# Up and down projections by seven block products in place of eight, with the bias table stored in parts and read back later

## What is computed

```python
def conv_ffn(x, w_up, conv_w, conv_b, w_down):     # x: 512 x 1024
    h = x @ w_up                                    # 1024 x 5632
    h = causal depthwise convolution of width 3 over the tokens, + conv_b
    a, u = jnp.split(h, 2, axis=-1)                 # 2816 columns each
    return (jax.nn.gelu(a, approximate=True) * u) @ w_down   # 2816 x 1024
```

## Time and profile before

| | us |
|---|---|
| median of 3 runs | 2482.78 (2482.14 to 2487.97) |
| the profiled execution, its own time | 2482.47 |
| its span, first to last instruction | 2480.5 |
| PE busy | 2371.9 (96%) |
| DVE busy | 895.6 (36%) |
| ACT busy | 572.9 (23%) |
| mean granted TensorE clock | 0.979 of full |

### The profile page before, as it was taken

How to read it: one execution, slowest core, us unless ns; L and a number is a source line. 1 busy time by engine, 2 the same in 40 slices (tenths; PEclk the granted TensorE clock), 3 DMA queues, 4 the chain that set the end, 5 groups by cost and what they waited for, 6 DMA issues and landing times.

```text
span 2480.5 us, 33541 instructions
## 1 busy us (share of the span) xinstructions
PE 2371.9 (96%) x13710; PEld 1195.7 (48%) x13710; DVE 895.6 (36%) x2187; ACT 572.9 (23%) x1211; POOL 0.2 (0%) x4
## 2 busy tenths in 40 slices
PE   7999999988999999989978999999899998999998
PEld 3555555564444444454434444444444655444553
DVE  6455555541522220034405222210236266131542
ACT  2222222212211110035513111100221253113550
POOL 0000000000000000000000000000000000000000
PEclk9999999979999999999989999999999998999998
DMA  3100000002212121111162212221112110111011
GB/s 113 47 31 31 31 31 31 19 19 104 84 68 85 68 97 70 70 43 43 43 124 102 85 69 83 70 91 70 57 68 83 54 35 35 68 68 63 31 43 68
DMA packets 25264, 154.56 MB, mean 62 GB/s; under 512 B 2476, under 2 KB 2604, under 8 KB 11308
## 3 DMA queue, kind: packets, MB, share of 16 engines
q1 hardware_dynamic: 22032, 145.57, 16.4%
q10 hardware_dynamic: 3100, 7.08, 1.6%
HBM read 146.61 MB, written 6.03 MB: 62 GB/s over the span
## 4 chain that ended last, share of the span: by engine, by line
PE 91%; DVE 5%; DMA 2%; issue 1%; ACT 1%; SPq 0%; DVEq 0%; ACTq 0%
PE banks L1384 23%; PE banks L1146 12%; PE banks L1057 8%; PE banks L1086 7%; PE banks L1744 4%; PE banks L470 3%; PE banks L438 3%; PE banks L1596 2%; PE banks L460 2%; PE banks L1630 2%; PE banks L1608 2%; PE banks L2328 2%; DMA arena<-o_attn 2%; PE banks L575 2%; PE banks L1399 1%
## 5 line engine op out<-in xcount | busy, mean ns | idle before, releaser
L1384 PE MATMUL banks<-arena 128*128 128x512 f32 x1344 | 577.7, 592 | 0.0
L1384 PEld LDWEIGHTS banks<-arena 128*128 128x128 f32 x1344 | 255.0, 190 | 319.6 <-issue 318.7
L1146 PE MATMUL banks<-arena 128*128 128x512 f32 x704 | 303.0, 591 | 0.0
L1439 DVE SCALAR_TENSOR_TENSOR arena<-banks,arena 128x511 f32<-128x511 f32 (+1 forms) x176 | 132.0, 750 | 387.4 <-ACT arena L1422 375.3
L1057 PE MATMUL banks<-arena 128*128 128x512 f32 x512 | 227.8, 606 | 14.6 <-DMA arena<-o_attn 14.6
L1146 PEld LDWEIGHTS banks<-arena 128*128 128x128 f32 x704 | 133.0, 189 | 169.7 <-issue 169.7
L1316 DVE TENSOR_TENSOR arena<-arena 128x512 f32<-128x512 f32 x70 | 48.3, 690 | 408.7 <-ACT arena L1275 405.2
L1422 ACT ACTIVATE arena<-banks,arena 128x512 f32<-128x512 f32 x88 | 68.1, 778 | 474.7 <-PE banks L1384 460.3
L1086 PE MATMUL banks<-arena 128*128 128x512 f32 x384 | 168.3, 595 | 0.0
L1057 PEld LDWEIGHTS banks<-arena 128*128 128x128 f32 x512 | 98.9, 195 | 141.1 <-issue 124.3
L1744 PE MATMUL banks<-arena 128*128 128x512 f32 x256 | 124.6, 614 | 0.0
(11 more groups left out here) (280 smaller groups left out, 2607.2 us busy)
## 6 DMA issues: line engine op xcount, KB each, us to landing
arena<-up SPq DMA_DIRECT2D x44, 1024.0 KB, 4.8
arena<-down SPq DMA_DIRECT2D x16, 1408.0 KB, 6.0
arena<-w_mix SPq DMA_DIRECT2D x8, 1728.0 KB, 7.4
arena<-e_in SPq DMA_DIRECT2D x12, 1024.0 KB, 4.8
arena<-o_in SPq DMA_DIRECT2D x8, 1024.0 KB, 4.8
arena<-w_o SPq DMA_DIRECT2D x4, 1024.0 KB, 4.8
arena<-q SPq DMA_DIRECT2D x8, 512.0 KB, 3.3
arena<-o_attn SPq DMA_DIRECT2D x4, 1024.0 KB, 14.8
```

The costliest lines, as they stand in the source:

```text
L1146: ins = pe.matmul(k.ps[:, j, :], k.ring[s][:, t * P:t * P + P], source[:, t, :], start=t == 0, stop=t == FT - 1)
L1384: ins = pe.matmul(k.ps[:, UP + 2 * s + m, :], k.ring[s][:, (m * KT + t) * P:(m * KT + t + 1) * P], source[:, t, :], start=t == 0, stop=t = ...
L1439: dve.scalar_tensor_tensor(conv[j][:, shift:T], k.ps[:, UP + j, 0:T - shift], k.vec("conv", col + tap), conv[j][:, shift:T], ALU.mult, ALU ...
```

## The change

**Up.** The first 4 slabs of a layer (`PLAIN`) stay as they are. The other 18 are computed by `seven_tensor`: the slab's weights are taken as 2 x 2 blocks (two output tiles by even and odd tiles of the contraction), the activations as 2 x 2 blocks (even and odd tiles by first and second half of the tokens), and seven products of blocks replace eight. Each product is 4 matmuls of 128x256. It needs four sums of weight blocks per slab (`weights_vector`, 128x512 each, DVE), four sums of activation blocks per layer (`turned_vector`, 128x1024 each, DVE), and copies of partial results from PSUM by ACT (`part_scalar`: five of 128x256 per slab), joined by DVE (three of 128x256 per slab). The convolution now reads rows in SBUF in place of PSUM.

**Down.** The class `Down` does the same for pairs of output tiles: four turns per layer, each seven products of 11 matmuls of 128x256. A turn needs both slots of the ring at once. DVE makes four sums of weight blocks of 128x1408 per turn, and, during up, `cross_vector` makes four sums of 128x256 of each pair of activation tiles. `TILES` no longer has the down projections; the bridge behind down squares the tiles in SBUF (`down_squared`).

**The first block's output projection** starts in the last pair: `out_tensor` puts 21 of the 64 matmuls of `w_o` in the places of the fill (8 in the levels, 13 in the scan), in banks 4, 5 and 3, and `tensor_begun` does the other 43.

**Attention.** `turned_tensor(s - 1)` moves ahead of `values_tensor(s - 2)`, in all three attention stages.

**Bias.** `bias_out` becomes four transfers of three rows each, issued by ACT behind each of the first four slabs of up in layer 1; `bias_in` moves behind the bridge after down in layer 1; `late_vector` goes behind the index scores of the third block, and the clearing of `idx` goes to the start of `even_in_vector`.

```diff
@@ class TimeMix
+    OUT = ([(0, t) for t in range(6)] + [(1, t) for t in range(6)] + [(m, 6) for m in range(2)] + [(2, t) for t in range(7)])
+    OUT_BANK = {0: 4, 1: 5, 2: 3, 3: 7}
+    def out_tensor(self, pe):
...
+        pe.wait_ge(self.tail_dve.sem, self.tail_dve.at(t, "gated"))
+        o = (m % 2 * KT + t) * P
+        ins = pe.matmul(k.ps[:, self.OUT_BANK[m], :], k.ring[m // 2][:, o:o + P], k.h[:, t, :], start=t == 0, stop=False)
@@ class Down
+        def product(n, bank, w, x, first, waits):
+            for t in range(FT // 2):
+                waits(t)
+                ins = pe.matmul(ps[:, bank, LO], w[:, t, :], x[:, t, :], start=first and t == 0, stop=t == FT // 2 - 1,
+                                skip_group_check=not first)
...
+            product("P1", 0, self.raw(0, 0), actv[:, 0::2, LO], True, even_ready)
...
+            product("P2", 2, self.raw(0, 1), actv[:, 1::2, LO], True, odd_ready)
...
+            product("P4", 3, self.raw(1, 1), self.t["T4"], True, cross_ready)
+            pe.wait_ge(A.sem, A.at(turn, "p1"))
+            pe.wait_ge(W.sem, W.at(turn, "S4"))
+            product("P6", 0, self.s["S2"], self.t["T2"], False, at_first)
...
+            product("P5", 1, self.s["S1"], self.t["T1"], True, at_first)
+            pe.wait_ge(A.sem, A.at(turn, "u2"))
+            product("P7", 0, self.s["S3"], self.t["T3"], False, at_first)
+            pe.wait_ge(A.sem, A.at(turn, "p5"))
+            product("P3", 1, self.s["S4"], actv[:, 1::2, HI], False, at_first)
@@ class ConvUp
+    def seven_tensor(self, pe, layer, i, s, first=False):
...
+        product("P1", y, a11, k.h[:, 0::2, LO], True)
+        pe.wait_ge(J.sem, J.at(layer, i, s - 2, "c11"))
+        pe.wait_ge(W.sem, W.at(layer, i, s, "S1"))
...
+        product("P5", xa, self.s["S1"], self.t[0], True)
+        pe.wait_ge(A.sem, A.at(layer, i, s, "p1"))
+        pe.wait_ge(W.sem, W.at(layer, i, s, "S2"))
...
+        product("P6", y, self.s["S2"], self.t[1], False)
+        pe.wait_ge(A.sem, A.at(layer, i, s, "p5"))
+        pe.wait_ge(W.sem, W.at(layer, i, s, "S4"))
+        product("P3", xa, self.s["S4"], k.h[:, 1::2, HI], False)
+        pe.wait_ge(A.sem, A.at(layer, i, s, "u2"))
+        pe.wait_ge(W.sem, W.at(layer, i, s, "S3"))
...
+        product("P7", y, self.s["S3"], self.t[2], False)
+        product("P2", xb, a12, k.h[:, 1::2, LO], False)
+        pe.wait_ge(A.sem, A.at(layer, i, s, "u3"))
...
+        product("P4", y, a22, self.t[3], False)
@@ ConvUp, ScalarE's order for one slab
+        if not first:
+            self.part_scalar(act, layer, i0, s0, "c21")
+            self.ident_scalar(act, layer, i0, s0, 0, conv)
+        self.part_scalar(act, layer, i, s, "p1")
+        if not first:
+            self.ident_scalar(act, layer, i0, s0, 1, conv)
+        self.part_scalar(act, layer, i, s, "p5")
+        if not first:
+            self.gelu_scalar(act, layer, i0, s0, conv)
+        self.part_scalar(act, layer, i, s, "u2")
+        self.part_scalar(act, layer, i, s, "u3")
@@ ConvUp, VectorE's order
+        with dve.Fori(0, SEVENS // 2 - 1) as i:
             for s in range(2):
...
+                self.weights_vector(dve, layer, i, s + 1)
+                self.seven_vector(dve, layer, i, s, conv)
+            self.cross_vector(dve, layer, i + PLAIN // 2)
@@ class Attend
             project(s)
+            if 1 <= s <= self.count:
+                self.turned_tensor(pe, s - 1)
             if s >= 2:
                 self.values_tensor(pe, s - 2, lambda n: free(s - 2, n))
-            if 1 <= s <= self.count:
-                self.turned_tensor(pe, s - 1)
@@ class Second
-        act.dma_start(bass.AP(self.scratch.ap().tensor, 0, [[P * 641, 12], [641, P], [1, 640]]),
-                      self.line[0:12, :].unsqueeze(1).broadcast_to([12, P, 640])).then_inc(self.scratch_stored, 16)
+        act.dma_start(bass.AP(self.scratch.ap().tensor, 3 * part * P * 641, [[P * 641, 3], [641, P], [1, 640]]),
+                      self.line[3 * part:3 * part + 3, :].unsqueeze(1).broadcast_to([3, P, 640])).then_inc(self.scratch_stored, 16)
@@ program
-            lin.tensor(pe, "w_o", k.h, 2, lambda t: pe.wait_ge(mix.tail_dve.sem, mix.tail_dve.at(t, "gated")))
+            lin.tensor_begun(pe, mix)
...
-            sec.bias_in(act)
-            up.scalar(act, 1, conv, bridge, 2)
+            up.scalar(act, 1, conv, bridge, 2, lambda part: sec.bias_out(act, part))
```

More of the change, by code:

```diff
@@ L655, in tensor, with last_fill @@
             more = n + 1 < PAIRS
+            def last_fill(count):
+                if not more:
+                    for _ in range(count):
+                        self.out_tensor(pe)
             def level_fill(lv, half):
@@ L1024, in stream @@
                          ).then_inc(k.landed[s], 16)
-TILES = {"w_o": 8, "down0": 8, "o_attn": 8, "down1": 8, "e_in": 28, "e_o": 8, "o_in": 24, "o_o": 8}
+TILES = {"w_o": 8, "o_attn": 8, "e_in": 28, "e_o": 8, "o_in": 24, "o_o": 8}
 BASE = {}
@@ L1069, in tensor, with tensor_begun @@
                 self.slab(pe, name, i, s, source)
+    def tensor_begun(self, pe, mix):
+        k, name = self.k, "w_o"
+        assert not mix.out_left
+        pe.wait_ge(mix.tail_dve.sem, mix.tail_dve.at(PAIRS - 1, "gated"))
+        for m in range(4):
+            for t in range(KT - 1 if m < 3 else 0, KT):
+                o = (m % 2 * KT + t) * P
+                ins = pe.matmul(k.ps[:, mix.OUT_BANK[m], :], k.ring[m // 2][:, o:o + P], k.h[:, t, :], start=t == 0,
+                                stop=t == KT - 1)
+                if m == 3 and t == 0:
+                    k.begun(ins, 1)
+            ins.then_inc(self.summed, 1)
+        for s in range(2):
+            self.slab(pe, name, 1, s, k.h)
     def landed_tensor(self, pe, name, n):
@@ L1425, in pair_scalar, with part_scalar @@
         act.activation(conv[2 * s], conv[2 * s], ACT.Gelu_apprx_tanh).then_inc(self.gelu, 1)
-    def scalar(self, act, layer, conv, bridge, n):
+    def part_scalar(self, act, layer, i, s, name):
+        A, S = self.parts, self.products
+        product, bank = {"p1": ("P1", 0), "p5": ("P5", 1), "u2": ("P6", 0), "u3": ("P7", 0), "c21": ("P4", 0)}[name]
+        act.wait_ge(S.sem, S.at(layer, i, s, product))
+        if name == "c21":
+            act.wait_ge(self.used, i * 2 + (2 + layer * FT + PLAIN + s))
+        A.done(act.activation(self.row[1][:, LO] if name == "c21" else self.part[name], self.k.ps[:, UP + 2 * (s % 2) + bank, LO],
+                              ACT.Copy), name)
@@ new lines, in weights_vector @@
+    def weights_vector(self, dve, layer, i, s, first=False):
+        k, S, W = self.k, self.products, self.weights
+        a11, a12, a21, a22 = self.raw(s % 2)
+        dve.wait_ge(k.landed[s % 2], i * 16 + (TURN[f"up{layer}"] + (PLAIN + s) // 2 + 1) * 16)
+        for name, x, y, op, own, use in (("S1", a21, a22, ALU.add, None, "P5"), ("S2", self.s["S1"], a11, ALU.subtract, "S1", "P6"),
+                                         ("S4", a12, self.s["S2"], ALU.subtract, "S2", "P3"),
+                                         ("S3", a11, a21, ALU.subtract, None, "P7")):
+            if own:
+                dve.wait_ge(W.sem, W.at(layer, i, s, own))
+            if not first:
+                dve.wait_ge(S.sem, S.at(layer, i, s - 1, use))
+            W.done(dve.tensor_tensor(self.s[name], x, y, op), name)
```

338 lines of the change are left out of this document (290 added, 48 removed).

## The result

The changed kernel takes 2408.5 us (median of 4 runs, 2407.9 to 2409.0) beside 2482.8 for the kernel before on the same chip: a ratio of 0.9693, 95% interval 0.9679 to 0.9706. It is faster, as forecast, by 74 us in place of 103; the time lies 5.5 us above the upper end of the range. The profiled execution has a span of 2406.8 us (2480.5 before).

The account below looks back on a forecast made before the run. TensorE was taken to set the time almost everywhere (91% of the chain that ended last). From 2482.5 us, -59.9 - 36.7 + 1.0 - 7.5 - 18.3 + 16 + 0.5 + 1.5 = -103.4 gave 2379 us, range 2356 to 2403.

Parts of the forecast that it names:

- Up and down, TensorE, with waits between products: Seven products for eight save 59.9 us in up and 36.7 in down over two layers; waits between products add 1.0.
- DVE and ACT fit under it: In up, new DVE and ACT work costs nothing; DVE needs 8.6 of 12.1 us a slab.
- down starts without a stall: At the start of down, weight sums end at 14 us, P6 is due at 14.25; cost 0, high 1 us twice.
- The rivals of costly waits: In up and down, waits of 0.14 us for each of 308 products cost 43 us, giving 2422; chance 0.08.
- DVE as the bound: In up, DVE sets the pace at 15.0 us a slab, giving 2483 or more; chance 0.03, including other losses that size.
- The projection begun in the last pair: First block: 21 of 64 `w_o` matmuls moved into the last pair save 7.5 us; low 5, high 12.
- The store taken away from `o_attn`: Without the bias store, `o_attn` loses its slab waits and runs like `w_o`: 18.3 us off.
- Attention order and the bias read back: Transposes ahead of values in attention add 1.5 us; reading the bias back beside slabs of `e_in` adds 0.5.
- The bias store put into up: In up of layer 1, four parts delay slabs on three engines: 16 us on, 5 to 35 likely; chance 0.55.
- Its pace of 0.25 to 0.3 us for a row's copy: Bias store in up of layer 1: 0.25 to 0.3 us per copy, the parts lasting some 130 us in all.

Follow-up runs that it names:

- sums done twice: 96-row kernel with each of the four sums of weight blocks per slab done a second time in both up projections; 2376.6 us, ratio 0.9558.
- the experiment: 96-row kernel with none of the output projection `w_o` begun in the last pair; 2369.1 us, ratio 0.9536.
- four-parts-of-12-rows kernel: Changed kernel with the four bias stores in the same places, each of 12 rows with 32 copies instead of 3 with 128; 2376.7 us, ratio 0.9579.
- no part is held: Changed kernel with all four parts in up of layer 1, spaced so each is issued when the one ahead has ended; 2398.2 us, ratio 0.9639.
- 96-row kernel: Changed kernel with the bias row on 96 partitions, stored ahead of `o_attn` by one transfer of 96 rows with 16 copies; 2364.4 us, ratio 0.9530.
- the one with ScalarE held by 22, 27 and 18 copies: 96-row kernel with ScalarE held in up of layer 1 by in-place copies (17.6, 21.7, 14.4 us), without transfers; 2408.8 us, ratio 0.9676.

## Why the prediction was wrong by 29 us

By its own steps, with starts of stages in the two traces:

- *Up and down, TensorE, with waits between products.* Predicted for a layer -29.9 - 18.4 + 0.5 = -47.8. From the start of up to the first matmul of the norm behind down in layer 0: 459.7 before, 411.9 after, -47.8. That a product's wait costs next to nothing, that DVE and ACT fit under it, and that down starts without a stall is right in both layers. The rivals of costly waits and of DVE as the bound are excluded; with sums done twice DVE still costs only 0.27 us a slab. Of DVE's operations the prediction counts 18 in a slab where its own list has 14 (4 + 3 + 4 + 1 + 2), as the kernel has; this changes neither the sum nor which way the rival fell.
- *The projection begun in the last pair.* Predicted -7.5. Up of layer 0 starts at 611.7 in place of 616.8, -5.1; the experiment gives 3.9 in the traces and 4.7 by the medians. So it lies at the low end of 5, or just under it.
- *The store taken away from `o_attn`.* Predicted -18.3. From its start to the start of up it is 82.8 before and 68.1 after: -14.7. No slab is late, but the clock is 0.5 from 1171.8 to 1185.4, over the stage's start, and again from 1240.0 to 1253.7. In the four-parts-of-12-rows kernel, which is the same up to there, the first of these stretches is missing and the second lasts 10.2 us; there the projection takes 55.3 us and the whole 64.8, 18.0 less than before, as predicted.
- *Attention order and the bias read back.* Predicted +2.0. Window stage -1.9, even with its input +0.1, the stage of `o_in` -1.5, latent +4.4: +1.1 in sum. The order's loss is there, but all of it in the latent stage.
- ***The bias store put into up.*** **This is the step that failed.** Predicted +16, 5 to 35 likely, by slabs alone; the issue of the parts on ScalarE's queue was costed at nothing. Measured: 47.8 - 7.5 = +40.3 in layer 1 between the same two places, 24 of the 29 us.

What stood in its place has two halves. The hold: 54 us of issues, which by themselves cost 36.6 us. The late slabs: by themselves 27 us when no part is held. Together they cost 39.6, not 64, because they overlap: while PE stands for ScalarE it takes no slab, and the slab that it would have waited for lands meanwhile. Each of the three is a run, the overlap is the reading of them, and the chain bears it out: it goes through 52.6 us of issues, and PE's wait of 6.8 for the slab (1294.1 to 1300.9) lies inside the second of them (1284.2 to 1301.5). The 27 us are of parts placed further apart than in the changed kernel; the four in their old places with no hold were not seen, since GpSimd's queue made another store of them.

The prediction's reading of the slabs was right in kind: 104 of a slab's packets pass at once and 24 wait, so three engines of 16 serve the store. Its pace of 0.25 to 0.3 us for a row's copy holds for the first part (35.8 us for 128 copies, 0.28); the four together took 109 us (0.21), where 130 was forecast. A copy takes 0.108 us at the median with the three rows apart, and 0.353 in the stores of twelve neighbouring rows; with three neighbours it takes 0.186 (the first part's median) or 0.353 (a quarter of that part's copies and more).

By the Trainium skill, "DMA: Bandwidth & Descriptors", section "Why a DMA increments its semaphore by 16 and not by 1", three rows use always the same three engines; the 24 packets agree. By "SBUF — State Buffer" of the Trainium skill, section on the port swizzle (Door 1), four neighbouring partitions share a port; the durations agree in kind, 0.108 us with one row at a port and 0.353 with four.

The 27 us of late slabs are within the step's 5 to 35, above its 16. With this alone the sum would have been 2390 and inside the range. That the issue of the whole store had taken 1.40 us before was the row that misled: it was one issue, with nothing under way ahead of it.

Why an issue lasts is read from rows, not shown by itself: it holds when each of its engines gets 128 copies and most of the 128 of the part ahead are not done; not when the part ahead has ended (0.72 us), not with 32 for each engine (0.30), not with 96 and nothing ahead (0.69); and with faster copies less (2.85, 7.12). A limit on how many copies can stand in an engine's queue would do all this. Where it lies no run was made to find. With the rows apart, where the three engines should keep step, the two held issues ended with 260 and 266 older copies unfinished, by an estimate 87 to 89 for each engine beside the 128 of its own; in the changed kernel, where the engines do not keep step, they ended with 146, 154 and 156.

## What to carry to other kernels

An issue is an instruction of the engine that makes it. When a transfer is cut in parts that follow each other on the same few engines, look at the length of the issue rows, not at the number of instructions, and ask what that engine owes to TensorE meanwhile. Before a transfer is hidden somewhere, make it short: spread it over more rows and with them over more engines. Here 96 rows with 16 copies each were worth 44 us, and the store costs its old place ahead of `o_attn` nothing. And when two stalls meet in one place, measure each by itself: their sum says little about what removing one of them gives.

## What the runs showed of the hardware that was not expected

- Issues of transfers of the same shape took from 0.72 to 21.9 us on ScalarE's queue, by what was under way ahead of them.
- A slab's packets on engines that serve a store wait behind many of its copies at a time: of the slab above the last packets went through in groups, 8 and then 16, with 3.6 and 4.5 us between, and not one by one between the copies. With the store's rows 8 partitions apart the slabs show no such groups: all 128 packets pass in one run of 5.6 to 7.2 us.
- Kernels that are the same up to there end the window stage with the clock at 0.5 for 13.7 us, from about 1172, or without it. The 96-row kernel and the one with ScalarE held by 22, 27 and 18 copies differ only behind that place: in the traced execution of the first that stretch is missing and up of layer 1 starts at 1242.5, in that of the second it is there and up starts at 1248.6. Other kernels fall to either side (1242.9 with four parts of 12 rows, 1248.05 in the changed one). That is 5 to 6 us from nothing in the program. It may be a good part of the scatter of up to 11 us in the runs of one kernel: of the held kernel the run of 2398.0 us has a mean clock of 0.977, those of 2409 have 0.970.
